# Second block's stage products with tokens on partitions, last weight rows tile by tile

## What is computed

```python
for i in range(DEPTH):                                  # DEPTH = 2, x is [1, 512, 1024]
    hn = rms_norm(x, norm_gains[i, 0])
    m = stick_breaking_attention(hn, ...) if i == 0 else dilated_attention(hn, ...)
    x = x + rms_norm(m, norm_gains[i, 1])
    f = conv_ffn(rms_norm(x, norm_gains[i, 2]), ffn_w_up[i], ffn_conv_w[i], ffn_conv_b[i], ffn_w_down[i])
    x = x + rms_norm(f, norm_gains[i, 3])

def rms_norm(x, g):      # over the 1024 channels of a token
    return x * lax.rsqrt(jnp.mean(x * x, axis=-1, keepdims=True) + EPS) * g
```

## Time and profile before

| | us |
|---|---|
| device time, median of 3 runs | 2281.8 |
| lowest and highest of them | 2281.36, 2284.24 |
| span of the profiled execution | 2283.8 |
| PE busy in it | 2138.7 |
| PE weight loads | 1640.1 |
| DVE busy | 1295.8 |
| ACT busy | 1031.5 |
| POOL busy | 133.7 |

### The profile page before, as it was taken

How to read it: one execution, slowest core, us unless ns; L and a number is a source line. 1 busy time by engine, 2 the same in 40 slices (tenths; PEclk the granted TensorE clock), 3 DMA queues, 4 the chain that set the end, 5 groups by cost and what they waited for, 6 DMA issues and landing times.

```text
span 2283.8 us, 31295 instructions
## 1 busy us (share of the span) xinstructions
PE 2138.7 (94%) x13216; PEld 1640.1 (72%) x13216; DVE 1295.8 (57%) x1837; ACT 1031.5 (45%) x1501; POOL 133.7 (6%) x112
## 2 busy tenths in 40 slices
PE   5979989999997998999889999998999998999997
PEld 4656654577765665777667888886877776888885
DVE  3567765666637775355536766435255546766533
ACT  3556641255625664377744433324333355433331
POOL 0011200000001210000010000003000002000000
PEclk9989999999997998999999999999999999999998
DMA  9999970022217984211012222221222112222210
GB/s 398 384 361 370 369 298 0 17 95 112 112 75 263 357 343 187 111 38 38 38 74 111 105 80 111 92 110 52 91 95 95 48 71 78 111 77 108 111 56 37
DMA packets 40571, 324.12 MB, mean 142 GB/s; under 512 B 7231, under 2 KB 8255, under 8 KB 21695
## 3 DMA queue, kind: packets, MB, share of 16 engines
q1 hardware_dynamic: 27288, 288.91, 32.8%
q0 software_dynamic: 10624, 25.71, 3.2%
q10 hardware_dynamic: 2512, 7.41, 0.8%
HBM read 310.40 MB, written 24.19 MB: 147 GB/s over the span
## 4 chain that ended last, share of the span: by engine, by line
PE 85%; DVE 7%; ACT 4%; DMA 2%; issue 2%; POOL 0%; SPq 0%; DVEq 0%; ACTq 0%; POOLq 0%
PE PS L163 80%; PE PS L891 2%; PE PS L641 1%; DVE work L2344 1%; ACT work L1591 1%; DMA work<-tokens,slots 1%; PE PS L1152 1%; DVE WR L2350 1%; ACT XH L1284 0%; ACT work L1596 0%; ACT L1596 0%; DMA work<-in_xtok 0%; ACT work L1587 0%; DVE work L2405 0%; DMA ring<-in_wexp 0%
## 5 line engine op out<-in xcount | busy, mean ns | idle before, releaser
L163 PE MATMUL PS<-HS,RS 128*128 128x512 f32 x4128 | 951.0, 391 | 9.4 <-DVE HS L2121 8.6
L163 PEld LDWEIGHTS PS<-HS,RS 128*128 128x128 f32 x4128 | 773.8, 188 | 175.3 <-issue 13.7
L1765 DVE TENSOR_TENSOR RS<-ring,RS 128x1024 fp32r<-128x1024 f32 x212 | 259.0, 1224 | 342.2 <-ACT RS L1248 342.2
L1248 ACT ACTIVATE RS<-ring 128x1024 fp32r<-128x1024 f32 x212 | 221.5, 1052 | 252.3 <-PE PS L163 252.3
L1688 ACT ACTIVATE work<-work,vec 128x512 f32<-128x512 f32 x88 | 71.9, 817 | 239.5 <-DVE work L2471 239.5
L1765 DVE TENSOR_TENSOR CR<-ring,WR 128x1024 fp32r<-128x1024 f32 x128 | 153.3, 1222 | 37.5 <-ACT WR L1248 35.0
L163 PE MATMUL PS<-work 128*64 128x128 f32 (+5 forms) x1728 | 131.9, 294 | 29.7 <-DVE work L1824 19.9
L1248 ACT ACTIVATE WR<-ring 128x1024 fp32r<-128x1024 f32 x128 | 134.8, 1058 | 51.3 <-PE PS L163 44.9
L163 PEld LDWEIGHTS PS<-work 128*64 128x64 f32 (+2 forms) x1728 | 107.7, 147 | 49.4 <-issue 31.0
L1248 ACT ACTIVATE work<-PS 128x384 f32<-128x384 f32 (+2 forms) x194 | 86.7, 484 | 116.2 <-PE PS L674 37.4
L163 PE MATMUL PS<-RS,HS 128*128 128x512 f32 x480 | 116.0, 400 | 8.3 <-DVE HS L2121 8.3
(11 more groups left out here) (256 smaller groups left out, 2793.1 us busy)
## 6 DMA issues: line engine op xcount, KB each, us to landing
ring<-in_wexp SPq DMA_DIRECT2D x32, 2048.0 KB, 10.6
ring<-in_wmod SPq DMA_DIRECT2D x24, 2048.0 KB, 11.2
ring<-in_ffnu SPq DMA_DIRECT2D x22, 2048.0 KB, 8.1
ring<-in_wexp SPq DMA_DIRECT2D x32, 1024.0 KB, 11.0
ring<-in_ffnd SPq DMA_DIRECT2D x10, 2048.0 KB, 7.2
ring<-in_dilqk SPq DMA_DIRECT2D x6, 2048.0 KB, 8.1
ring<-in_sbqk SPq DMA_DIRECT2D x4, 2048.0 KB, 8.0
ring<-in_dilv SPq DMA_DIRECT2D x3, 2048.0 KB, 8.0
```

The source lines that it names most:

```text
L163: return T.matmul(out, l, r, start=start, stop=stop, skip_group_check=True)
L1248: return S.activation(out, x, ACT.Copy, **kw)
L1765: V.tensor_tensor(lo, src, hi.bitcast(F32), ALU.subtract).then_inc(w_lo, 1)
```

## The change

1. The four stage products are turned: tokens are on the output's partitions. The stationary operand is 128 tokens of the attention's or the ffn's output, the moving one 512 output channels of a row of weights (`row_products`). The 8 banks hold 4 tiles of 128 tokens by 2 halves of the channels.
2. `close` goes over rows of weights as before in the ffn, for the attentions too, but leaves the last ones (2 of 8, 4 of 22, 2 of 4, 4 of 22) apart and does those tile by tile, so tiles finish one after another. All rows left apart have to be split and held at once; so the next stage's first units get places in `work` (`head` of `stream`), and the last row of the dilated product too (`last`).
3. Norms go along rows: ACT squares a tile's two banks with an accumulated sum, DVE multiplies the banks by a gain row held on all partitions (a DMA by POOL, `gains`), then a root, a reciprocal and one add of 128x1024 into x, which is now kept as tokens by channels (`XN`). POOL's adds, the copies to `HL`, the `stat_add` matmuls and the spreads for these norms are gone: 56 `stat_add` and 7 spreads in all. Three spreads of another form remain, for the norms before the next stages.
4. x is turned back for the next stage by PE: 16 transposes for two tiles (`turn_pair`), the first pair before the last tile's products, the second after two units of the next stage. Once, before the stick attention's output product, x itself is turned to rows by 32 transposes, copied by ACT and DVE.
5. The next stage's first units (3, 4, 3) are done by halves of 256 tokens (`first_units`), so they can begin when half of `HS` is there. In the dilated stage these are four units of q and k, which now come before V.
6. Before the last head pair of the stick attention PE does 2 `mm3` of the output product, not 6.
7. The result is stored by SP in four DMAs of 128 tokens, as tiles finish.

```diff
@@ -299,29 +301,39 @@
     ring.restart(4)
     stream("stick", [(("sbv", n), A["sbv"][n], 4096, by_rows(8, 512), 4) for n in range(2)] +
            [(("sbqk", n), A["sbqk"][n], 4096, by_columns(8, 512), 4) for n in range(4)] +
-           [(("sbo", n), A["sbo"][n], 4096, by_columns(8, 512), 4) for n in range(2)], 3, 3)
-    stream("ffn0", ffn_units(0), 5, 3, 5, (2, 0, 1, 3, 4), (2, 1, 0, 0, 0))
-    stream("dil", [(("dilv", n), A["dilv"][n], 4096, by_rows(8, 512), 4) for n in range(3)] +
-           [(("dilqk", n), A["dilqk"][n], 4096, by_columns(8, 512), 4) for n in range(6)] +
-           [(("dilo", 0), A["dilo"], 4096, by_columns(4, 1024), 4)], 2, 2, 2, None, (4, 3))
-    stream("ffn1", ffn_units(1), 5, 3, 5, (2, 0, 1, 3, 4), (2, 1, 0, 0, 0))
+           [(("sbo", n), A["sbo"][n], 4096, by_rows(4, 1024), 4) for n in range(2)], 3, 3)
+    stream("ffn0", ffn_units(0), 5, 3, 5, (2, 0, 1, 3, 4), (2, 1, 0, 0, 0), (("work", 2048), ("work", 8192)))
+    qk_units = [(("dilqk", n), A["dilqk"][n], 4096, by_columns(8, 512), 4) for n in range(6)]
+    stream("dil", qk_units[:1] + [(("dilv", n), A["dilv"][n], 4096, by_rows(8, 512), 4) for n in range(3)] + qk_units[1:] +
+           [(("dilo", 0), A["dilo"], 4096, by_rows(4, 1024), 4)], 2, 2, 2, None, (2, 1),
+           (("ring", 4), ("work", 2048), ("work", 8192)), 6144)
...
-        def out_products(first, kc, src_of, base, c, bank, some):
-            per = 8 // kc
-            key, src, hi, lo, before = parts(first + c // per)
-            pe.wait_ge(w_lo, first + c // per + 1)
-            s = slice(c % per * 128, c % per * 128 + 128)
-            for k in some:
-                pe.wait_ge(f_l, base + k + 1)
-                x = mm3(PS[:, bank, :], (hi[:, k, s], lo[:, k, s]), src_of(k), k == 0, k == kc - 1)
+        def turn_pair(i, P):
+
+            pe.wait_ge(ro_x, 4 * i + 2 * P + 2)
+            for e in range(8):
+                c = ORDER[i][e]
+                for t in (0, 1):
+                    x = T.transpose(PS[:, (4, 0)[P] + e // 2, (e % 2 * 2 + t) * 128:(e % 2 * 2 + t) * 128 + 128],
+                                    XN[:, 2 * P + t, c * 128:(c + 1) * 128], ident)
+                x.then_inc(ro_t, 1)
+
+        def row_products(p, src, ready, k, kc, tiles, free=None):
+
+            key, w, hi, lo, before = parts(p)
+            pe.wait_ge(w_lo, p + 1)
+            ready(k)
+            for b in tiles:
+                t = (b // 2 + 2) % 4
+                if free:
+                    free(b)
+                s, h = slice(t * 128, t * 128 + 128), slice(b % 2 * 512, b % 2 * 512 + 512)
+                x = mm3(PS[:, b, :], [v[:, s] for v in src(k)], (hi[:, 0, h], lo[:, 0, h]), k == 0, k == kc - 1)
             return x
 
-        def project_out(first, kc, src_of, base, po, call, banks, made=0):
-            per = 8 // kc
-            for c in range(8):
-                pe.wait_ge(po_c, po + c - 1)
-                x = out_products(first, kc, src_of, base, c, banks[c], range(0 if c else made, kc))
-                x.then_inc(w_done if c % per == per - 1 else po_half, 1)
-                if c:
-                    stat_add(call, c - 1)
-            stat_add(call, 7)
-            stat_spread(call)
+        def close(a, first, kc, apart, src, ready, free, banks=range(8), made=()):
+
+            for k in range(kc - apart):
+                some = [b for b in banks if (b, k) not in made]
+                row_products(first + k, src, ready, k, kc, some, free if k == 0 else None).then_inc(w_done, 1)
+            for t in range(4):
+                for k in range(kc - apart, kc):
+                    x = row_products(first + k, src, ready, k, kc, (BANK[t], BANK[t] + 1))
+                    if t == 3:
+                        x.then_inc(w_done, 1)
+                if t < 3:
+                    x.then_inc(ro_m, 1)
+                if t == 2 and a < 3:
+                    turn_pair(a + 1, 0)
+
+        def first_units(i, first):
+
+            n_units = FIRST_UNITS[i]
+
+            def products(u, P):
+                key, src, hi, lo, before = parts(first + u)
+                pe.wait_ge(w_lo, first + u + 1)
+                for n in range(8):
+                    k = ORDER[i][n]
+                    pe.wait_ge(nm_l, 8 + pair_count(i, P, n if P else max(n, 2 * u + 1)))
+                    x = mm3(half(i, P, PS[:, 4 + u, :]), (hi[:, k, :], lo[:, k, :]), [half(i, P, v) for v in hs(k)],
+                            n == 0, n == 7)
+                if P:
+                    x.then_inc(w_done, 1)
+
+            products(0, 0)
+            products(1, 0)
+            turn_pair(i, 1)
+            for u in range(2, n_units):
+                products(u, 0)
+            for u in range(n_units):
+                products(u, 1)
+                if u == 1:
+                    pe.wait_ge(st_rcp, 8 + i)
+                    for t in range(4):
+                        x = mm(PS[:, 3, t * 128:t * 128 + 128], next_rs[:, t:t + 1].to_broadcast([128, 128]), ident, True, True)
+                    x.then_inc(st_bc, 1)
 
         def stick():
             first = part_of["stick"].start
@@ -1087,6 +1179,13 @@
                     for h in range(2):
                         i = mm(o[h][:, c:c + L], v(n, h), Tz[h][:, a:a + L], False, n == 2)
                 i.then_inc(sk_v, 1)
+
+            def out_of(k):
+                return OR[:, k, :], OL[:, k, :]
+
+            def out_ready(k):
+                pe.wait_ge(sk_q, 8)
+                pe.wait_ge(f_l, 8 + k + 1)
 
...
         def dilated():
             first = part_of["dil"].start
+            first_units(2, first)
+            pe.wait_ge(rb_c, 3)
+            for r in range(4):
+                x = T.transpose(PS[:, 3, r * 128:(r + 1) * 128], RB[2][:, r * 128:(r + 1) * 128], ident)
...
+        def out_root(a, t, done):
+
+            act.wait_ge(*done)
+            for h in range(2):
+                if h:
+                    act.wait_ge(ro_h, 8 * a + 2 * t + 1)
+                if t:
+                    act.wait_ge(*rows_squared(a, "out", f"{t - 1}{h}"))
+                S.activation(spent[:, h * 512:h * 512 + 512], PS[:, BANK[t] + h, :], ACT.Square,
+                             accum_out=out_sq[:, h, t:t + 1]).then_inc(sq_act, 1)
+            act.wait_ge(ro_a, 4 * a + t + 1)
+            S.activation(out_rs[:, t:t + 1], out_rs[:, t:t + 1], ACT.Sqrt, bias=C("eps"), scale=1.0 / 1024).then_inc(st_sqrt, 1)
+
+        def next_square(a, t):
+            act.wait_ge(ro_x, 4 * a + 4 + t + 1)
+            S.activation(XO[:, t, :], XN[:, t, :], ACT.Square, accum_out=next_rs[:, t:t + 1]).then_inc(sq_act, 1)
+
+        def next_hi(i, P, e):
+            c = ORDER[i][e]
+            act.wait_ge(ro_t, 8 + pair_count(i, P, e | 1))
+            copy(half(i, P, HS[:, c, 0, :]), turned_half(i, P, e), scale=gain(i, c)).then_inc(nm_h, 1)
+
+        def next_part(a, last, after):
+
+            i = a + 1
+            table(0)
+            for t in range(2):
+                out_root(a, t, (ro_m, 3 * a + t + 1))
+            next_square(a, 0)
+            out_root(a, 2, (ro_m, 3 * a + 3))
+            for e in range(8):
+                if e > 3:
+                    act.wait_ge(w_done, last)
+                next_hi(i, 0, e)
+            out_root(a, 3, (w_done, last))
+            for t in (1, 2):
+                next_square(a, t)
+            for e in range(8):
+                next_hi(i, 1, e)
+            next_square(a, 3)
+            act.wait_ge(*rows_squared(a, "next", 3))
+            S.activation(next_rs, next_rs, ACT.Sqrt, bias=C("eps"), scale=1.0 / 1024).then_inc(st_sqrt, 1)
+            split_hi(after, part_of[after].start + len(STREAM[after][6]) + 2)
+            act.wait_ge(st_bc, 8 + (1, 2, 4)[a])
+            copy(rows_out(i, RB[i]), rows_in(i, PS[:, 3, :])).then_inc(rb_c, 1)
 
         def project_rows(name, i, dst, b0, columns):
             first = part_of[name].start
@@ -1552,24 +1712,8 @@
             for t in range(4):
                 copy(dst(t), PS[:, b0 + t, :], scale=rcol[:, t:t + 1]).then_inc(pr_c, 1)
...
-        def transition(a, name, late):
-
-            rcp(8 + 2 * a)
-            split_lo(name, part_of[name].start + (2 if a == 1 else 3))
-            dve.wait_ge(st_bc, 9 + 2 * a)
-            dve.wait_ge(*((fd_ca, 4) if a == 1 else (po_c, 4 * a + 8)))
-            for n, c in enumerate(ORDER[a + 1]):
-                if n > 3:
-                    dve.wait_ge(an_xp, 8 * a + n - 3)
-                g = ((0, 1), (0, 3), (1, 1))[a]
-                V.scalar_tensor_tensor(out=W(13312 + n % 4 * 512, 512), in0=HL[:, c, :],
-                                       scalar=VC("ng", (g[0] * 4 + g[1]) * 8 + c, 1),
-                                       in1=PS[:, 2, :], op0=ALU.mult, op1=ALU.mult).then_inc(an_t, 1)
-                if n > 1:
-                    rows_lo(a + 1, n - 2)
-                if n == 6:
-                    split_lo(name, late[0])
-            rows_lo(a + 1, 6)
-            rows_lo(a + 1, 7)
```

(55 more changed lines are left out.)

393 lines of the change are left out of this document (200 added, 193 removed).

## The result

The changed kernel takes 2244.45 us, the median of 4 runs (2240.74 to 2247.6); the kernel before took 2282.01 beside it. The ratio is 0.983, with an interval of 0.982 to 0.984. The forecast was 2256.4 with a range of 2247 to 2269: the sign is right, the gain too small, 37.6 us where 25.4 were forecast.

The account below looks back on a forecast made before the run. PE is busy 2138.7 of 2283.8 us, so only its waits and needless work at the stage ends can be won. Gains 2.2 + 8.7 + 0.8 + 13.7 = 25.4 us from 2281.8 give 2256.4, range 2247 to 2269.

Parts of the forecast that it names:

- Pace: PE's matmul prices: 0.2275 us at 512 columns, 0.134 at 256, so a half unit 3.22; ten units by halves +9.7 us.
- Rival 1: Narrow matmuls are paced by their weight loads, 0.198 us each: 30.7 us on top, 2287.1, slower; chance 0.05 in full.
- late wait: PE's wait before the fourth half unit in the dilated hand-over, for a split on DVE: 4.8 us, plus 1.6 for the clock.
- First ffn to dilated stage: From the first ffn's rows left apart to the first dilated scores: 140.3 us to 139.5, a gain of 0.8.
- Rival 3: Strided half-chunk reads in the dilated stage are as cheap as without stride (0.48), clock stays up: 4.9 us, 2251.5; chance 0.12.
- rival 2: The dilated stage's strided half-chunk reads are dearer from PSUM than from SBUF, 0.5 us more each: +6 us, 2262.4; chance 0.13.
- Stick product to first ffn: From the last head pair's values to unit 3 of the first ffn: 75.5 us to 73.3, a gain of 2.2.
- dilated product to second ffn: From the dilated output product to unit 3 of the second ffn: 57.2 us to 48.5, a gain of 8.7.
- rival 5: The hand-overs give nothing, as DVE and ACT become what is late; only the end gains: 2268.1; chance 0.04.
- Price of a tile's norm: At the stage ends, 3.4 us from ACT's first square to a tile of x, DVE doing tiles one after another.
- Rival 4: The tile's norm takes 1 us more, in the hand-overs and at the end: +8, 2264.4; chance 0.11.
- The end: From ACT's first square of the last banks to the span's end: 20.4 us becomes 3.4 plus a 3.3 store, gaining 13.7.

Follow-up runs that it names:

- narrow_twice: Changed kernel with the second token halves' products in the first units done twice, 240 more 256-column matmuls; 2270.31 us, ratio 0.994.
- store_once: Changed kernel with the result stored by one DMA of 2048 KB behind the last tile, not four of 512 KB; 2246.7 us, ratio 0.985.
- stride_in_sbuf: Changed kernel with the dilated stage's half chunks read from their bank in order and written to `HS` with the stride; 2246.26 us, ratio 0.984.
- one_row_apart: Changed kernel with only the last row of weights done tile by tile, in place of 2, 4, 2 and 4 rows; 2262.8 us, ratio 0.992.
- whole_units: Changed kernel with the next stage's first units at full width, after both pairs of tiles are turned; 2259.7 us, ratio 0.990.

## Why the prediction fell short

**What bounds the kernel.** Right. Nearly all of the gain lies at the four stage ends; the stretches between them moved by 0.1, -1.3 and 0.5 us.

**Pace: the step that failed first.** A half unit was put at 24 x 0.134. It is 24 x 0.120, as the row of 96 in `narrow_twice` shows. The 0.134 came out of a subtraction, 12 narrow matmuls within a row of 24 whose wide ones were assumed at 0.2275, and seemed to be confirmed by twelve transposes. With narrow ones at 0.120 the same row would have its wide ones at (4.20 - 11 x 0.120) / 12 = 0.240, an estimate near the 0.242 that the forecast itself read in the old dilated product; the row can't tell the two apart. Nor did the twelve transposes hold for others: the kernel after does 16 in (1.97 - 0.27) / 15 = 0.113. The argument had a bound above (0.198) and none below, though half of the wide pace, 0.114, was there to be read. Rival 1 is refuted by the same rows. Of the 480 narrow matmuls 72 stand ahead of the late wait and only shift it, so 408 x 0.014 = 5.7 us. The transposes and the spreads give about 3.5: 0.8 for the first 32, 0.4 each for four groups of 16 and the one of the dilated hand-over that lies on the path, 0.2 for each of three spreads. Against it, the turned product goes at 0.232 in the stick stage and in the tiles of the dilated one (1.39 us from one row of six to the next) and not at 0.2275: some 1.1 us lost over the 258 of its matmuls that lie on the path.

```profile
1861.39 1.55 PE L164 MATMUL PS<-RS 128*128 128x512 f32 x6
1862.78 1.56 PE L164 MATMUL PS<-WR,RS 128*128 128x512 f32 x6
```

These are the 3.1 us too few in the stick hand-over and the 2.7 in the second.

**First ffn to dilated stage: the step that failed most.** Forecast 0.8 with bounds of 5 gained to 6 lost; it is 9.4, outside of them. V starts 53.5 us behind the rows left apart and not 62.2, and from there to the scores all is as forecast, 77.4 for 77.3. The strided half chunk was priced by a read out of SBUF (0.72 on ACT, 0.70 on DVE); out of PSUM the eight follow each other at (3.02 - 0.48) / 7 = 0.36 us on ACT and (3.22 - 0.48) / 7 = 0.39 on DVE, no dearer than without a stride. One record is still 0.48 long:

```profile
L1363 ACT ACTIVATE HS<-PS,vec 128x256 fp32r<-128x256 f32 x48 | 18.4, 480 | 7.5 <-PE PS L164 6.9 <-PE PS L1050 0.6
```

Eight chunks take ACT 3.0 us for 6.0, and the four ahead of the first half unit save 1.8: 4.8 us. With that and faster transposes the late wait is 2.50 for 4.8. In the profiled execution the clock stayed up behind it, 1.6 us more, which makes 6.4; that part is luck, since behind the same wait it fell in `store_once` and `narrow_twice`. Rival 3 had the mechanism, with a chance of 0.12, but with a chunk at 0.48, the length of a record and not the pace of a row, and with a clock that stays up below 3 us, which those two runs don't bear out. The forecast's own row was near in its stride and far in the memory that is read. `stride_in_sbuf` shows that the stride is free on PSUM's side and not on SBUF's, and rival 2 falls with it.

**Stick product to first ffn; dilated product to second ffn.** The chain of steps is right, one wait of 1.35 for 1.7 included, and `one_row_apart` and `whole_units` show that the rows left apart and the halves each carry what was said; rival 5 is refuted. Only the prices of the paragraph on the pace were off.

**Price of a tile's norm.** Right: 3.44 us for 3.4. The accumulated square brings an instruction that no row of before had in this place, `ACTIVATION_READ_ACCUMULATOR`, 0.19 us each; it lies beside DVE's products. Rival 4 is refuted.

**The end.** 14.3 for 13.7. The store of 512 KB took 2.6 us, near the half of the earlier trace rows and not 3.3.

**The account.** Of 15.4 us missed by spans: narrow matmuls 5.7, transposes and spreads 3.5, the strided chunks with the wait 4.8, the clock that stayed up there 1.6, the store 0.6, other stretches 0.3 (1.0, 0.1 and 0.5 gained, 1.3 lost at the scores), the turned product -1.1. The 1.0 ahead of the change, the 1.3 and the 1.6 differ between executions. But for the turned product the errors of price had all one sign: each was put too dear, so they added up instead of cancelling. The range went down to 2247 and closed above 2244.45.

**What is open.** What brings the clock down. It stayed up behind every wait of 1.35 us, fell behind those of 3.71, 4.12, 5.35 and 5.98, and behind 2.5 us in the late wait and 2.99 at the scores it did either, with the same instructions. What PE had done before those waits was not varied. Why the executions of after are slower ahead of the values' end, where nothing was edited, is open too; the traces show it for the profiled ones alone.

## What to carry to other kernels

Where a term is multiplied by some hundreds of instructions, bound its price from both sides: 0.014 us was 6 us here. A row that was got by subtraction is no better than the assumption subtracted, and half of the wide one's pace would have been the other bound. Take the price of a strided access from a row with the same memory on the same side, not from one with the same stride. Take the pace from a row of many and not from the length of one record: 0.36 and 0.48 us here. Price the clock's fall behind a wait of 2 to 3 us as a chance and not as a yes or no: the same wait cost 1.3 to 1.6 us more in one execution and nothing in the next. To compare kernels that share their first half, begin at the point where they part. Doing the first work of the next stage by halves of the tokens is nearly free here (0.240 us a pair for 0.2275) and covers a tile's norm.

## What was not expected of the hardware

A 128x256 matmul with its own weight load goes at 0.120 us in a row of 96, though each load's record is 0.188 long. Reading PSUM with a stride of 4 elements costs neither ACT nor DVE anything (1.55 us for four half chunks either way), while writing SBUF with that stride costs 0.54 us a chunk for 0.38. Stores by SP take 2.6 us for 512 KB and 6.6 us for 2048 KB. Behind the same wait of 2.5 us, with the same instructions, the granted clock stayed at 1.00 in one execution (after) and fell to 0.50 in another (`store_once`).
